# First expert pass gathered from a list made of the ranks alone; gate rows loaded behind the last weights

## The chip, the cores and the metric

The kernel runs on one core of a Trainium2 chip. The metric is the device time of one execution in microseconds (us).

## What is computed

One inference step of a two-layer trunk over 640 tokens (128 context, 512 latent), width 1024, all in fp32. Every layer mixes tokens (mLSTM, windowed attention, neighbourhood attention), adds and normalises, and then runs a mixture of experts:

```python
pg = softmax(x @ w_rg); grp = argmax(pg)            # 1 of 4 groups
top_l, top_i = top_k(le_of_that_group, 2)           # 2 of its 8 experts
out = (silu(xb @ w_g[e]) * (xb @ w_u[e])) @ w_d[e]  # 1024 -> 256 -> 1024, 32 experts
y = segment_sum(out * w, token, 640)
x = layer_norm(ALPHA * x + gate_f * y, g, b)
```

The change lies in the routing and in the start of the experts, once in each layer.

## The kernel before

**The experts.** Each layer streams all 32 experts' weights from HBM: every expert has a gate, an up and a down piece of 1 MB each. Experts 0 to 3 have a fixed place (64 rows each): passes 0 and 1 hold two each. The others are ordered by how many tokens chose them, and passes 2 to 16 take one or two of them each. Last comes a loop for what overflows (one turn in this run) with four experts' pieces. The 96 pieces of a layer go through 18 slots of SBUF in one fixed order. SyncE (SP) issues them all on one DMA queue (`piece`, L752 to L761); before a piece it waits until TensorE is done with the piece that held the slot. Pieces 0 to 11 are those of passes 0 and 1; pieces 12 to 14 wait for the experts' order (`ctl`); piece 15 waits for the token weights (`w12`, made after the token lists) and for the landing of the first gather (`gath0`), since its slot lies over tiles of the routing. Piece 16 is split in two halves. Piece 17 waits for `x1` of the last token tile, which GpSimd makes. Piece 18 and the following wait for passes 0, 1, ... in turn: 18 and 19 for the gates of pass 0, 20 and 21 for its ups, 27 for the downs of pass 1.

**A pass.** For pass b GpSimd gathers 128 token rows from HBM (`gather`, L3016) by a list of token numbers `gidx`, one column a pass; TensorE turns them (`block_x`, L1513), ScalarE and VectorE copy one half each to SBUF, TensorE makes gates and ups (`block_gates_ups`, L1532), turns the hidden values (L1563) and makes the downs (`block_down`, L1553); GpSimd scatters the rows by `sidx` (L3029). In program order TensorE does gates and ups of pass b, then the turning of pass b+1, then the downs of pass b-1.

**The routing,** ahead of pass 0, is one chain between VectorE and TensorE. VectorE picks the experts of the last token tile. TensorE counts (job RK: every token's rank in its expert). VectorE finds which expert outranks which (`outrank`), TensorE sums (RR), VectorE gives each expert its place, TensorE spreads it (RB). VectorE then computes each token's pass and slot (`hot["pass"]`, `hot["slot"]`), TensorE turns these into lists (RX, L1489, 10 matmuls), VectorE makes `gidx` and `sidx` of them (`lists`, L2646 to L2654), TensorE puts `sidx` in order for light passes (RQ, L1498). Between these jobs TensorE runs `keep_busy(16)` twice (L882), matmuls whose result nobody reads. ScalarE fills the gather's target with zeros ("nought", L1910) when all rows of h2, the experts' input, have been stored to HBM (`st_h2`); GpSimd waits for `st_h2`, `nought` and `lists`, then gathers for pass 0 and pass 1. VectorE, after its lists, makes the token weights (`weights_of_two`, L2523 to L2530), one `ln_gain` (L2383) and the overflow numbers (L2667 to L2678).

**The gate rows.** The gate of the second residual, `m["gf"]`, is two rows of 1024 numbers, each broadcast to 128 partitions (512 KB written each). GpSimd loads them in pass PASSES - 2 = 15. They are used after the last pass, in `combine`.

Of the kernel before, what the change touches and what calls it, by code (L numbers as in the profile page):

```python
# [21 lines left out]
P = 128  # L22
# [245 lines left out]
for _stage, _steps in (  # L268
        ("cond", ("sig_c", "silu_c", "maskb", "hmod", "modT", "arows", "arow", "acol")),
# [4 lines left out]
        ("route", ("r_ge", "r_ed", "r_gd", "r_dl", "assign", "hot", "ctl", "outrank", "place", "wx", "logits", "w12"))):  # L274
# [146 lines left out]
def program(nc, A, table):  # L421
    ev = Events(table)
    with ExitStack() as ctx:
# [115 lines left out]
        hot["past"] = region(att, 3524, 1, MAXOVF, NE)  # L539
        s5 = region(small, 0, P, 20, NT)  # L540
# [92 lines left out]
        def x_turned(b_, half):  # L633

            out, src = e["xT"][:, parity(b_), half * 512:(half + 1) * 512], bank[half][:, :]
            if isinstance(b_, int) and b_ < PASSES and pass_kind(b_) == "heavy":
                return out, src
# [80 lines left out]
        def _(eng):  # L718
# [9 lines left out]
            for l in range(DEPTH):  # L728
# [60 lines left out]
                for i in range(12, len(PIECES) - 3 * QUAD):  # L789
# [9 lines left out]
                    elif i == 15:  # L799
                        eng.wait_ge(*ev.at("w12", l))  # L800
# [9 lines left out]
                with eng.Fori(0, more) as i:  # L810
                    src = [expert(i * QUAD + (LOOP0 + c)) for c in range(QUAD)]
                    for q, free in enumerate(("quad_gates", "quad_ups", "quad_downs")):
                        eng.wait_ge(W[free], now(Count(i, 1, 1)))
                        for c in range(QUAD):
                            piece(PASSES, c, q, src[c])
                eng.wait_ge(W["out_psum"], now(Count(more, 1, PASSES)))
# [21 lines left out]
        def _(eng):  # L838
# [145 lines left out]
            for l in range(DEPTH):  # L984
# [489 lines left out]
                last.then_inc(*jobs.filled())  # L1474
                bk = jobs.open("RB", l)
# [6 lines left out]
                keep_busy(16)  # L1482
                bk = jobs.open("RX", l)
                eng.wait_ge(*jobs.room())
                for k in range(2):
                    eng.wait_ge(*ev.at("hot", l, k))
                    for t in range(NT):
                        n = k * NT + t
                        last = eng.matmul(bk[:, 0:NLIST], hot["slot"][:, n, :], hot["pass"][:, n, :], start=(n == 0),  # L1489
                                          stop=(n == 2 * NT - 1))  # L1490
                last.then_inc(*jobs.filled())


                bk = jobs.open("RQ", l)
                eng.wait_ge(*jobs.room())
                eng.wait_ge(*ev.at("lists", l))
                for c_ in range(QUAD):
                    last = eng.matmul(bk[c_ * UNIT:(c_ + 1) * UNIT, 0:NLIST], by_entry(ident)[:, 0, c_, :],  # L1498
                                      r["t1"].rearrange("p t n -> p (t n)")[:, 0:NLIST], start=True, stop=True)
                last.then_inc(*jobs.filled())  # L1500
                W = MOE[l]
                for n in range(jobs.n - BANKS, jobs.n):
                    eng.wait_ge(*ev.at("free", n))
# [1618 lines left out]
```

## Time and profile before

| | us |
|---|---|
| three runs | 1553.67, 1550.94, 1554.16 (median 1553.67) |
| profiled execution, its own time | 1554.2 |
| span of the profiled execution | 1552.4 |
| TensorE busy | 1419.2 (91%) |
| VectorE / ScalarE / GpSimd busy | 610.6 / 335.2 / 366.5 |
| granted TensorE clock, mean | 0.963 of full |
| mean DMA rate over the span | 240 GB/s |

The experts' part of layer 0 lies at 485 to 757 us of the span, that of layer 1 at 1236 to 1508. DMA rates in a stretch are given as the mean busy share of the 16 DMA engines and as GB/s. All times below are from the span's start.

### The profile page before, as it was taken

To read this page: it belongs to the slowest core of one execution; us is meant where nothing else is said; L and a number is where in the kernel's file an instruction comes from. 1 tells how busy PE (TensorE), PEld (TensorE's weight loads), DVE (VectorE), ACT (ScalarE), POOL (GpSimd) and SP (SyncE) were. 2 spreads that over 40 slices of the span, in tenths; PEclk is the share of its full clock that TensorE was granted. 3 is DMA by queue.
4 is the path that set the end of the run, shared out by engine and by line. 5 is a ranking of instruction groups with operands and counts; after the bars stand their busy time and mean duration, and the time that the engine had idled before them with its cause. 6 is when DMAs were issued, how large, how long until landed. Compare 5 with 4: busy or idle time off the path is not lost.

```text
span 1552.4 us, 25254 instructions
## 1 busy us (share of the span) xinstructions
PE 1419.2 (91%) x9681; PEld 1089.8 (70%) x9681; DVE 610.6 (39%) x1453; ACT 335.2 (22%) x853; POOL 366.5 (24%) x471
## 2 busy tenths in 40 slices
PE   6999999898998999996899999989888989999974
PEld 5889898675887766563488889876577876656441
DVE  1121333578278322211352124348746852211216
ACT  2211211464111111110141111236420111111102
POOL 0100006542451312111010000744237321121101
PEclk9999999999998999999999999999999989999987
DMA  9420111675817999999642111147442499999974
GB/s 378 129 65 33 65 62 39 214 278 201 329 65 281 373 381 420 418 418 418 248 127 72 58 65 33 68 152 260 172 173 117 164 359 386 420 418 418 417 292 170
DMA packets 76741, 355.37 MB, mean 229 GB/s; under 512 B 20464, under 2 KB 23792, under 8 KB 43088
## 3 DMA queue, kind: packets, MB, share of 16 engines
q1 hardware_dynamic: 43056, 292.66, 47.7%
q0 software_dynamic: 20416, 46.73, 8.3%
q10 hardware_dynamic: 13152, 14.37, 2.8%
q8 instruction: 79, 1.29, 0.3%
q14 instruction: 38, 0.31, 0.1%
HBM read 341.25 MB, written 32.07 MB: 240 GB/s over the span
## 4 chain that ended last, share of the span: by engine, by line
PE 75%; DVE 8%; DMA 8%; issue 4%; POOL 3%; ACT 1%; SPq 1%; ACTq 0%; DVEq 0%; POOLq 0%
PE bank L1167 22%; PE bank L1532 15%; PE bank L1553 7%; DMA ring<-in_w_exp 4%; PE bank L1403 4%; PE bank L956 2%; PE bank L1151 2%; PE bank L1326 2%; PE bank L859 2%; DMA att<-mod_rows 2%; PE bank L1513 2%; PE bank L1300 1%; PE bank L1113 1%; PE bank L1116 1%; PE bank L882 1%
## 5 line engine op out<-in xcount | busy, mean ns | idle before, releaser
L1167 PE MATMUL bank<-ring,hT 128*128 128x256 f32 (+1 forms) x1600 | 340.9, 373 | 1.1 <-DVE z L2243 1.1
L1167 PEld LDWEIGHTS bank<-ring,hT 128*128 128x128 f32 x1600 | 292.9, 191 | 38.1 <-issue 1.6
L1532 PE MATMUL bank<-z,att 128*64 128x256 f32 (+2 forms) x960 | 181.1, 397 | 11.6 <-DMA ring<-in_w_exp 11.2
L1532 PEld LDWEIGHTS bank<-z,att 128*64 128x64 f32 (+2 forms) x960 | 118.7, 151 | 50.2 <-DMA ring<-in_w_exp 12.2
L1403 PE MATMUL bank<-ring,hT 128*128 128x256 f32 x640 | 142.5, 381 | 1.7 <-ACT hT L1839 1.1
L1403 PEld LDWEIGHTS bank<-ring,hT 128*128 128x128 f32 x640 | 120.7, 191 | 17.8 <-issue 2.0
L2694 DVE TENSOR_TENSOR att<-att,bank 128x256 f32<-128x256 f32 x36 | 15.2, 421 | 273.2 <-ACT att L1928 273.2
L3029 POOL DMA_INDIRECT expert_rows<-att,cur x36 | 37.1, 1031 | 358.5 <-DVE att L2707 349.4
L1532 PE MATMUL bank<-ring,att 128*64 128x256 f32 (+2 forms) x672 | 117.0, 413 | 3.4 <-issue 1.9
L1532 PEld LDWEIGHTS bank<-ring,att 128*64 128x64 f32 (+2 forms) x672 | 71.1, 146 | 21.2 <-issue 4.1
L2243 DVE COPY z<-bank 128x512 f32<-128x512 f32 (+3 forms) x35 | 20.2, 578 | 152.5 <-PE bank L1167 152.5
L1553 PE MATMUL bank<-ring,att 128*64 128x512 f32 (+2 forms) x240 | 72.8, 597 | 6.8 <-DVE att L2713 4.9
L1687 ACT ACTIVATE z<-bank 128x512 f32<-128x512 f32 (+2 forms) x37 | 19.0, 516 | 266.2 <-PE bank L1167 249.4
L1854 ACT ACTIVATE att<-bank,sm 128x384 f32<-128x384 f32 (+2 forms) x100 | 55.4, 559 | 86.0 <-DVE sm L2308 45.1
L1928 ACT ACTIVATE att<-bank 128x256 f32<-128x256 f32 x36 | 13.8, 383 | 269.2 <-PE bank L1532 269.2
L2707 DVE COPY att<-bank 128x512 f32<-128x512 f32 x36 | 24.9, 692 | 109.6 <-PE bank L1553 109.6
L2305 DVE TENSOR_REDUCE sm<-bank 128x1 f32<-128x384 f32 (+2 forms) x100 | 50.4, 532 | 27.3 <-PE bank L1272 16.3
L1532 PE MATMUL bank<-hT,att 128*64 128x256 f32 (+2 forms) x240 | 51.0, 396 | 7.3 <-DMA z<-in_w_exp 6.9
L2852 POOL TENSOR_TENSOR att<-z,const 128x64 f32<-128x64 f32 x64 | 23.7, 400 | 140.2 <-ACT z L1687 139.1
L1553 PEld LDWEIGHTS bank<-ring,att 128*64 128x64 f32 (+2 forms) x240 | 22.4, 140 | 43.1 <-issue 36.3
L3016 POOL DMA_INDIRECT att<-h_rows,att x36 | 37.7, 1047 | 59.8 <-DVE att L2654 24.3
L1300 PE MATMUL bank<-const,att 128*128 128x128 f32 x284 | 41.4, 280 | 8.4 <-DVE att L2329 7.2
(407 smaller groups left out, 2367.9 us busy)
## 6 DMA issues: line engine op xcount, KB each, us to landing
z<-in_w_exp SPq DMA_DIRECT2D x74, 1024.0 KB, 22.3
ring<-in_w_exp SPq DMA_DIRECT2D x72, 1024.0 KB, 23.0
ring<-in_w_ada SPq DMA_DIRECT2D x41, 1024.0 KB, 6.5
ring<-in_w_in SPq DMA_DIRECT2D x24, 1024.0 KB, 5.0
hT<-in_w_exp SPq DMA_DIRECT2D x24, 1024.0 KB, 28.8
att<-in_w_exp SPq DMA_DIRECT2D x12, 1024.0 KB, 7.4
ring<-in_w_out SPq DMA_DIRECT2D x8, 1024.0 KB, 9.8
z<-expert_rows ACTq DMA_DIRECT2D x16, 512.0 KB, 8.9
```

Source lines behind the costliest of these rows:

```text
L859: last = eng.matmul(ada_ps[32 * j:32 * j + 32, P:P + UN], cond_at(m, 2 * j + kk), w[:, 2 * j + kk, :], start=(m == 0 and kk == 0), stop=(m ...
L956: last = eng.matmul(bk[:, i * UN:(i + 1) * UN], hTv[:, k, t * P:(t + 1) * P], w[:, k, :], start=(i == 0 and k == 0), stop=(k == KD - 1), s ...
L1151: last = eng.matmul(bk[:, i * UN:(i + 1) * UN], hTv[:, k, t * P:(t + 1) * P], ws[n][:, k, :], start=(k == 0), stop=(k == KD - 1))
L1167: last = eng.matmul(bk[:, i * UN:i * UN + nw], hTv[:, k, t * P:(t + 1) * P], w[:, k, 0:nw], start=(k == 0), stop=(k == KD - 1))
L1300: last = eng.transpose(bk[:, j * P:(j + 1) * P], c["p"][:, i % 3, s, j * P:(j + 1) * P], ident)
L1403: last = eng.matmul(bk[:, i * UN:(i + 1) * UN], hTv[:, k, t * P:(t + 1) * P], w[2 * half + i][:, k, :], start=(k == 0), stop=(k == KD - 1))
L1532: last = eng.matmul(bank[2 + j][c * m_:(c + 1) * m_, u * DE:(u + 1) * DE], rows, wv[c][k // 4][:, k % 4, :], start=(k == 0), stop=(k == KD ...
L1553: last = eng.matmul(bank[5 + half][c * m_:(c + 1) * m_, :], e["hmT"][:, j, k * P + c * m_:k * P + (c + 1) * m_], wv[c][k][:, half * 512:(h ...
L1854: eng.activation(c["p"][:, i % 3, s, 0:nk], bk[:, 0:nk], ACT.Exp, bias=sm[:, 0, u:u + 1], accum_out=sm[:, 1, u:u + 1]).then_inc(*jobs.free ...
L2305: eng.tensor_reduce(sm[:, 0, 2 * i + s:2 * i + s + 1], bk[:, 0:nk], AX, ALU.max).then_inc(*dve.step())
L3016: eng.indirect_dma_start(e["xg"][:, j, :], None, h2_dram[l], bass.IndirectOffsetOnAxis(ap=col, axis=0), bounds_check=last_row(b_, NTOK), o ...
L3029: eng.indirect_dma_start(y_dram[l], bass.IndirectOffsetOnAxis(ap=cur[:, 2 + j:3 + j], axis=0), e["ob"][:, j, :], None, bounds_check=last_r ...
```

## The change

- VectorE: `rows_shifted` of the last tile (its sum is the last rows of h2) goes ahead of the copy of RK. After `outrank` four new instructions build `hot["first"]`: for the fixed experts 0 to 3 a token's slot in passes 0 and 1 follows from its rank alone. TensorE's new job RF (5 matmuls of one column) turns the part for pass 0 into a list, and VectorE writes it to `cur[:, 0:1]` (two instructions): this is the event `first_rows`.
- GpSimd's gather of pass 0 takes `cur` in place of `gidx`, and waits for `first_rows` and the first half of `nought`; that of pass 1 waits for the other half and for `lists`.
- TensorE: one of the two `keep_busy(16)` is gone. RX and RQ leave the eight-bank job order and use fixed columns of bank 7. RX (`token_lists`) now stands behind the turning of pass 0, RQ (`lists_in_order`) between its gates and its ups.
- Pass 0's rows are not put in the four-way order of light passes, and ScalarE copies both halves of them.
- VectorE: weights, `ln_gain` and the first two overflow instructions stand ahead of the three that finish `sidx`; the rest of the overflow work follows. The event is now `sidx`.
- SP: piece 15 waits for `sidx` in place of `w12`. ScalarE's sigmoid of pass 0 and the first scatter wait for `sidx` too.
- The gate rows are issued by SP behind the last weight piece.

```diff
                     elif i == 15:
-                        eng.wait_ge(*ev.at("w12", l))
+                        eng.wait_ge(*ev.at("sidx", l))
                         eng.wait_ge(W["gath0"], 16)
...
                             piece(PASSES, c, q, src[c])
+                done, count = after(POOL_OF[l][2])
+                eng.wait_ge(W[done], count)
+                eng.wait_ge(*ev.at("st_modr", l))
+                for g in range(2):
+                    eng.dma_start(m["gf"][:, g, :], rows[at:at + D].partition_broadcast(P))
...
+                bk = jobs.open("RF", l)
+                eng.wait_ge(*ev.at("hot_first", l))
+                for t in range(NT):
+                    last = eng.matmul(bk[:, 0:1], hot["first"][:, t, :, :].rearrange("p c j -> p (c j)"), K["idv"][:, t:t + 1],
+                                      start=(t == 0), stop=(t == NT - 1))
...
                         last.then_inc(W["gu" if u else "gate"], 1)
+                        if u == 0 and isinstance(b_, int) and b_ == 0:
+                            lists_in_order()
...
                 keep_busy(16)
                 block_x(0)
+                token_lists()
                 n = passes(eng, l, one_pass, turn)
...
-                for t in range(NT):
-                    eng.wait_ge(*ev.at("st_h2", l, t))
                 eng.wait_ge(*ev.at("assign", l, 1))
                 for j in range(2):
+                    if j:
+                        for t in range(NT):
+                            eng.wait_ge(*ev.at("st_h2", l, t))
...
+                rows_shifted(NT - 1)
                 bk = jobs.bank("RK", l)
...
-                rows_shifted(NT - 1)
+                place_first = r["th"][:, :, 0:2]
+                for c_ in range(2):
+                    last = eng.scalar_tensor_tensor(out=place_first[:, :, c_], in0=r["rk"][:, 0:NT, c_], scalar=float(c_ * CAP - P),
+                                                    in1=r["ma"][:, :, c_], op0=ALU.add, op1=ALU.mult)
+                for c_ in range(2):
+                    last = eng.tensor_tensor(hot["first"][:, :, c_, :].rearrange("p t (h m) -> p t h m", h=2), ...)
+                last.then_inc(*dve.event("hot_first", l))
...
+                overflow_units()
+                lists_sorted()
+                overflow_turns()
                 n = passes(eng, l, one_pass, turn)
...
+                eng.wait_ge(*ev.at("nought", l, 0))
+                eng.wait_ge(*ev.at("first_rows", l))
                 gather(0)
+                eng.wait_ge(*ev.at("nought", l, 1))
+                eng.wait_ge(*ev.at("lists", l))
                 gather(1)
```

TensorE's order from RR to pass 0's ups, layer 0, before (L1473 RR, L1478 and L1480 RB, L882 keep_busy, L1489 RX, L1498 RQ, L1513 turning, L1532 gates and ups):

```order
L1480 MATMUL bank<-const,att 1x32
L882 MATMUL bank<-const 128x128 x16
L1489 MATMUL bank<-att 128x30 [waits dve_route,bank_free2]
...
L1498 MATMUL bank<-att,const 32x30 [waits bank_free2,bank_free3]
L1498 MATMUL bank<-att,const 32x30 x3
...
L882 MATMUL bank<-const 128x128 x15
L1513 MATMUL bank<-const,att 128x128 [waits gath0_0]
L1513 MATMUL bank<-const,att 128x128 x7
L1532 MATMUL bank<-ring,att 64x256 [waits slot_full2,slot_full3,xT_dve_0,xT_act_0]
L1532 MATMUL bank<-ring,att 64x256 x15
L1532 MATMUL bank<-z,att 64x256 [waits ring_full9,ring_full8]
```

The same stretch now (L893 keep_busy, L1528 turning, L1509 RX, L1516 RQ, L1547 gates and ups):

```order
L893 MATMUL bank<-const 128x128 x15
L1528 MATMUL bank<-const,att 128x128 [waits gath0_0]
L1528 MATMUL bank<-const,att 128x128 x7
L1509 MATMUL bank<-att 128x30 [waits dve_route]
...
L1547 MATMUL bank<-ring,att 64x256 [waits slot_full2,slot_full3,xT_dve_0,xT_act_0]
L1547 MATMUL bank<-ring,att 64x256 x15
L1516 MATMUL bank<-att,const 32x30 [waits dve_route]
L1516 MATMUL bank<-att,const 32x30 x3
L1547 MATMUL bank<-z,att 64x256 [waits ring_full9,ring_full8]
```

RX stood ahead of the first turning; it now stands behind it, and so behind the wait for the first gather; RQ stands behind the gates.

VectorE's order from the end of the lists to the overflow numbers, layer 0, before (L2661 to L2663 finish `sidx`, L2523 to L2530 weights, L2383 `ln_gain`, L2667 on overflow):

```order
L2654 TENSOR_TENSOR att<-att 128x30
L2657 COPY att<-att 1x32
L2661 CAST att<-bank 128x2 [waits bank_full3]
L2662 CAST att<-bank 128x3x3
L2663 CAST att<-bank 128x13
L2523 TENSOR_REDUCE small<-att 128x5 [waits act_route]
...
L2383 TENSOR_TENSOR x<-x,z 128x1024 [waits ld_ln1,act_norm,dve_route]
L2667 TENSOR_TENSOR att<-att,const 1x1280
L2669 TENSOR_REDUCE att<-att 1x40 [waits dve_step]
```

And now (L2708 to L2710 finish `sidx`):

```order
L2700 COPY att<-att 1x32
L2547 TENSOR_REDUCE small<-att 128x5 [waits act_route]
...
L2407 TENSOR_TENSOR x<-x,z 128x1024 [waits ld_ln1,act_norm,dve_route]
L2714 TENSOR_TENSOR att<-att,const 1x1280
L2716 TENSOR_REDUCE att<-att 1x40 [waits dve_step]
L2708 CAST att<-bank 128x2 [waits pe_cond,dve_step]
L2709 CAST att<-bank 128x3x3
L2710 CAST att<-bank 128x13
L2721 TENSOR_SCALAR att<-att 1x40
```

The three casts have moved behind the weights, `ln_gain` and two instructions of the overflow.

## Rows read from the trace of the kernel before

**Rows 1.** Stretches of layer 0: us, busy by engine, clock, DMA share, GB/s

```profile
556.00:640.00 84.00, 83.10 (x537) 50.63 (x537) 16.51 (x33) 10.66 (x20) 16.81 (x23) 1.00 1.02 419
640.00:740.00 100.00, 84.36 (x578) 49.53 (x578) 17.38 (x35) 11.04 (x21) 15.99 (x23) 0.96 1.02 418
745.00:750.00 5.00, 3.57 (x34) 2.00 (x38) 1.37 (x3) 0.60 (x1) 0.00 (x0) 1.00 0.05 18
```

**Rows 2.** Chain that ended last, end of layer 0: start, us, what

```profile
705.29 32.48 DMA ring<-in_w_exp
...
747.74 3.67 PE bank L1553 x32
```

**Rows 3.** SP's issues of pieces, layer 0: start, us from first to last

```profile
496.08 2.00 SPq L761 DMA_DIRECT2D z<-in_w_exp  x3
509.52 0.33 SPq L761 DMA_DIRECT2D att<-in_w_exp  x1
546.64 1.44 SPq L761 DMA_DIRECT2D hT<-in_w_exp  x2
```

**Rows 4.** Stretches of 2 and 4 us in layers 0 and 1, as group 1

```profile
544.00:546.00 2.00, 2.00 (x12) 0.57 (x8) 0.00 (x0) 0.00 (x0) 0.00 (x0) 1.00 0.73 297
546.00:548.00 2.00, 2.00 (x13) 1.48 (x10) 1.02 (x2) 0.60 (x1) 0.00 (x0) 1.00 0.33 66
548.00:550.00 2.00, 2.00 (x11) 1.77 (x10) 0.00 (x0) 0.00 (x0) 1.62 (x2) 1.00 0.85 332
...
1296.00:1298.00 2.00, 2.00 (x11) 0.44 (x7) 0.00 (x0) 0.00 (x0) 0.00 (x0) 1.00 0.64 258
1298.00:1300.00 2.00, 2.00 (x13) 1.79 (x11) 1.02 (x2) 0.60 (x1) 0.30 (x1) 1.00 0.48 92
```

**Rows 5.** Chain, start of layer 0's experts: start, us, what

```profile
500.78 2.40 PE bank L1489 x20
503.20 0.20 DVE att L2646
...
504.05 0.10 DVE att L2654
...
505.15 6.24 PE bank L882 x32
511.38 0.89 PE bank L1513 x8
...
513.81 7.14 PE bank L1532 x64
```

**Rows 6.** GpSimd's timeline, layer 0: start, us, what, idle before it and its releaser

```profile
492.48 0.53 POOL L2805 DMA_DIRECT2D h_rows<-att  x1 [7.80 <-DVE att L2430]
505.10 1.10 POOL L3016 DMA_INDIRECT att<-h_rows,att  x1 [12.09 <-DVE att L2654]
507.95 5.12 POOL L2956 TENSOR_TENSOR x<-x,z 128x1024 f32<-128x1024 f32 x2
```

**Rows 7.** DMA issues at 492 to 493, 505 and 514 to 516: KB, us to landing

```profile
h_rows<-att POOLq DMA_DIRECT2D x1, 512.0 KB, 7.3
...
att<-h_rows,att POOLq DMA_INDIRECT x1, 4.2
...
att<-h_rows,att POOLq DMA_INDIRECT x1, 8.2
```

**Rows 8.** VectorE's timeline, layer 0

```profile
490.98 1.20 DVE L2430 TENSOR_TENSOR att<-att 128x1024 f32<-128x1024 f32 x1
...
505.81 1.22 DVE L2383 TENSOR_TENSOR x<-x,z 128x1024 f32<-128x1024 f32 x1
...
508.46 1.47 DVE L2669 TENSOR_REDUCE att<-att 1x40 f32<-1x1280 f32 x1
```

**Rows 9.** keep_busy alone (TensorE, weight loads, clock, DMA), at either clock

```profile
485.00:488.00 3.00, 2.03 (x16) 1.87 (x16) 1.00 1.03 382
495.00:500.00 5.00, 5.00 (x25) 5.00 (x25) 0.50 1.00 365
```

**Rows 10.** The gate rows' issue in pass 15 of layer 0: KB, us to landing

```profile
z<-mod_rows POOLq DMA_DIRECT2D x2, 512.0 KB, 12.3
```

More of the change, by code:

```diff
@@ L1503, in _, with token_lists, lists_in_order @@
                     eng.wait_ge(*ev.at("free", n))
+                def token_lists():
+                    for k in range(2):
+                        eng.wait_ge(*ev.at("hot", l, k))
+                        for t in range(NT):
+                            n = k * NT + t
+                            last = eng.matmul(list_ps["all"], hot["slot"][:, n, :], hot["pass"][:, n, :], start=(n == 0),
+                                              stop=(n == 2 * NT - 1))
+                    last.then_inc(*pe.event("rx", l))
+                def lists_in_order():
+                    eng.wait_ge(*ev.at("lists", l))
+                    for c_ in range(QUAD):
+                        last = eng.matmul(list_ps["sorted"][c_ * UNIT:(c_ + 1) * UNIT, :], by_entry(ident)[:, 0, c_, :],
+                                          r["t1"].rearrange("p t n -> p (t n)")[:, 0:NLIST], start=True, stop=True)
+                    last.then_inc(*pe.event("rq", l))
                 def block_x(b_):
@@ L2590, in _ @@
                 eng.wait_ge(*dve.last())
+                bk = jobs.bank("RF", l)
+                eng.wait_ge(*jobs.full("RF", l))
+                none = r["th"].rearrange("p t g -> p (t g)")[:, 2:3]
+                eng.tensor_scalar(none, bk[:, 0:1], 0.0, float(FAR), ALU.is_equal, ALU.mult).then_inc(*dve.step())
+                eng.wait_ge(*dve.last())
+                eng.scalar_tensor_tensor(out=cur[:, 0:1], in0=bk[:, 0:1], scalar=-1.0, in1=none, op0=ALU.add,
+                                         op1=ALU.add).then_inc(*jobs.freed("RF", l))
+                ev.table[("first_rows", l)] = ev.table.get(("free", jobs.number(("RF", l))))
                 bk = jobs.bank("RB", l)
@@ L2653, in _ @@
                 eng.tensor_copy(sidx[:, :], lx)
-                eng.tensor_tensor(gidx[:, :], lx, lfar, ALU.add).then_inc(*jobs.freed("RX", l))
-                ev.table[("lists", l)] = ev.table.get(("free", jobs.number(("RX", l))))
+                eng.tensor_tensor(gidx[:, :], lx, lfar, ALU.add).then_inc(*dve.event("lists", l))
                 eng.tensor_copy(hot["inc"], inc[0:1, :])
-                bk = jobs.bank("RQ", l)
-                eng.wait_ge(*jobs.full("RQ", l))
-                lights = lambda ap: ap[:, 2:PASSES].rearrange("p (k i) -> p k i", k=GROUPS)[:, :, 2:5]
```

108 lines of the change are left out of this document (57 added, 51 removed).

## The prediction

> **What bounds the kernel now.** I looked for where the experts' part of a layer ends, then for what starts it. The stretches of layer 0 [rows 1] show the 16 DMA engines at a share of 1.02 and 418 to 419 GB/s from 556 to 740 us, without a break, and at 0.05 from 745. TensorE is busy for 84 of the 100 us from 640 to 740: it waits for weights. The chain that ended last says the same [rows 2]: a transfer issued at 705.29 lands 32.48 us later, and only the last downs (3.67 us at 747.74) come behind the last weights. So from 556 on the layer ends when a fixed number of bytes is through, however early TensorE starts its first pass. What moves the end is idle time of the DMA engines before 556, and bytes that stand ahead of the last weights.
>
> Idle time is in two places. At the start SP issues pieces 12 to 14 at 496.08 and piece 15 only at 509.52 [rows 3]. Later piece 27 is issued at 546.64, when pass 1's downs have freed its slot; the shares around it are 0.73, 0.33 and 0.85 [rows 4]: (0.27 + 0.67 + 0.15) x 2 = 2.2 us idle. There the stream has caught up with TensorE, so a stream that starts late can get back these 2.2 us and no more. In layer 1 it is (0.36 + 0.52) x 2 = 1.8 us.
>
> **The change, part by part.**
>
> *The first gather.* `rows_shifted` (1.20 us at 490.98 [rows 8]) moves ahead of the copy of RK and of three short instructions, 0.85 us earlier (491.0 to 490.1). The last h2 store, issued at 492.48 [rows 6], landed 7.3 us later [rows 7], at 499.8; it should land at 498.9. `first_rows` is no limit: four VectorE instructions and RF's five matmuls end near 495.5. Between its releaser (the lists, 504.15 [rows 5]) and its own start (505.10 [rows 6]) GpSimd's gather took 0.95 us, so the first gather starts at 499.9 and not at 505.1: 5.2 us earlier.
>
> *Its landing.* Before, it took 4.2 us, issued when the weight queue was nearly empty; the third, issued into a full queue, took 8.2 [rows 7]. Now pieces 12 to 14 are issued about 1.7 us later than before, from 497.7 to 499.4, so they are in the queue in front of it. (The trace has no row for the four new VectorE instructions ahead of RB. The smallest in it takes 0.10 us [rows 5], the largest 1.47 [rows 8]; at 5 and 320 columns I take 0.35 each, 1.4, and 0.3 for RF ahead of RB on TensorE.) I take 7.2, nearer to the full queue: 507.1. Bounds: 504.1 and 508.1. TensorE's one `keep_busy`, which now starts near 496 and takes 6.2 us [rows 5], is over by then.
>
> The Trainium skill ("DMA: Bandwidth & Descriptors", "Queues, rings and completion order") says that each DMA engine takes its queues in turn, packet by packet. By that the gather would get about half of 420 GB/s at once and land some 1.3 us later than on an empty queue, near 505.4; piece 15 would be issued 1.7 us earlier in each layer and the sum below would come out 3.4 us lower. The 8.2 us of the third gather are nearer to waiting behind what is queued, so the measured row is used.
>
> *The lists.* TensorE turns pass 0 (0.89 us after 511.38) and then makes RX (2.40 us) [rows 5]. Both rows are at the full clock, 2.4 GHz. TensorE has idled since 502.5 by then, and in the stretch after its last wait of this kind the granted clock was 0.50, 1.2 GHz: there a pass of `keep_busy` took 5.00 / 25 = 0.20 us against 2.03 / 16 = 0.13 [rows 9]. So 3.3 us become up to 5.1; I take 4.3 with hand-overs: RX ends at 511.4. The lists are ready 504.15 - 503.18 = 1.0 later, 512.4.
>
> *The event `sidx`.* This is the added wait. Behind the lists VectorE does weights, `ln_gain` (1.22) and two overflow instructions (1.47 each [rows 8]) before it finishes `sidx`. Before, from the lists (504.15) to the end of L2669 (509.93) it was 5.8 us, of which 0.9 was RQ's wait and the three casts; TensorE's `keep_busy`, which waited for these, began at 505.15 [rows 5]. That leaves 4.9, and with the casts (0.5) `sidx` comes at 512.4 + 5.4 = 517.8. RQ itself stands behind pass 0's gates: 511.4 + half of 7.14 [rows 5] + 0.4 = 515.4, not the last. SP issues piece 15 at about 518.0: **8.5 us later** than at 509.52, though the pass it serves has its rows earlier. Behind it in SP's queue stand all later pieces. Piece 17 also waits for `x1`: GpSimd's two `ln_shift` (5.12 us [rows 6]) behind the second gather, near 519, no later than its turn. Pieces 18 to 21 would have been free at 515 to 520.
>
> *From the wait to the end of the layer.* The 8.5 us are idle time of the queue, less what is absorbed: 2.2 us at piece 27 (1.8 in layer 1), and 0.6 for half of a gather (512 KB at 420 GB/s is 1.25 us), since the second gather now falls into the gap. The downs of pass 1, which free piece 27's slot, stay where they are: pass 0's gates start at 511.4 instead of 513.8, but the third gather now waits for overflow numbers that come after `sidx`, and takes that back. The stream reaches piece 27 near 553, so it isn't TensorE that it waits for. Added: 8.5 - 2.2 - 0.6 = 5.7 in layer 0, 6.1 in layer 1.
>
> *The gate rows.* Their 1.05 MB stood in the stream ahead of the last weights (issued in pass 15, landed in 12.3 us [rows 10]); at 419 GB/s that is 2.5 us in each layer. Behind the last weights they move when the engines are otherwise idle (share 0.05 [rows 1]), and land near 751, before `combine` needs them at 766. If that cover were gone they would cost their 2.5 us again. Gain: 2.5 a layer.
>
> *At nothing:* the dropped `keep_busy` (TensorE waits for the gather anyway), ScalarE's second half of pass 0 (0.6 us, beside RX on TensorE), and RF and the four VectorE instructions for it (1.7 us on the routing chain, which now ends at a wait for the gather; their cost is the later start of pieces 12 to 14, and the queue is still full from piece 11 then, or idles under 1 us, which I leave to the range).
>
> **The sum:** layer 0: 5.7 - 2.5 = +3.2; layer 1: 6.1 - 2.5 = +3.6; together +6.8, against the profiled execution's 1554.2: 1561.0. The median of the runs is 0.5 below that execution, so 1560.5.
>
> Bounds of it: with the first gather landing at 504.1 and the full clock, piece 15 is issued 3.0 + 1.0 earlier, at 514.0, and the sum is 6.8 - 8.0 = -1.2. With 508.1 and the low clock throughout it is 1.0 + 0.8 later: +3.6, so +10.4. That is 1552.5 to 1564.1.
>
> **The rivals.**
>
> *The gap closes (faster).* If piece 15 goes out by 512.4, within the 2.8 us that the later catching-up absorbs, the start costs nothing and only the gate rows are left: -5.0, 1548.7. For it: the gather starts 5.2 us earlier. Against: even at its best the way from landing to `sidx` is 3.3 + 1.0 + 5.4 = 9.7 us, so it would have to land by 502.6, 2.7 us after its start; no row is that short. The point from which it decides is this landing.
>
> *No change.* The early gather finds the queue as the first one did and lands in about 4.2 to 5.5 us. The late `sidx` and the gate rows cancel: -1.2 to +3, 1552.5 to 1556.7. The skill's rule on queues taken in turn would lead here.
>
> *Far slower.* TensorE becomes the bound of the start: a third gather issued behind the late overflow numbers, at 522 instead of 514.85, lands 8.2 us later, at 530 to 532, and holds the turning of pass 2; if that carried through to piece 27 beyond 553, idle time came back there. It would add some 3 us a layer: 1566. Against: that turning stood at 530 before, so it slips by 2 us, and the stream has 6 in hand.
>
> *It doesn't do what it says.* Pass 0 doesn't start earlier, since the gather meets the weights: its gates start at 513 to 514 as before, `sidx` is at 519.5. That is the upper bound, 1564.
>
> **How the numbers follow.** A measurement of this kernel tells about 0.2%, 3.1 us, from no change: below 1550.6 is faster, above 1556.8 slower. The forecast with its upper bound and the doesn't-do-it case has 0.54, far slower 0.06; no change 0.24; faster 0.16, more than the landing time alone would give it, since the stream's catching-up is read from one execution. The range, 1549.0 to 1565.0, takes in the bounds and half of the faster case.
>
> **What would show it.** Right: the first gather starts near 500 and lands near 507; piece 15 is issued at 517 to 519 and behind it no dip of the DMA share at 546; a DMA share far below 1 from about 509 to 519; the last downs of layer 0 some 3 us later; gate rows landing behind the last weights. Wrong: piece 15 before 514, or the gap there and the dip at 546 both still present, or a DMA share under 1 between 560 and 740, which would make TensorE the bound.

## The result, and the profile after

The change makes the kernel slower: median 1569.33 us (1568.51 to 1573.6, 6 runs) against 1552.31 (1549.1 to 1555.16, 6 runs of the kernel before), a ratio of 1.0109 [1.0093, 1.0125], so +17.0 us. Forecast were +6.8 us, and a range that ended at 1565.0. The sign and the wait that costs the time were right. The size was not: three terms of the way to that wait were too small, and one of them left out a cause. The profiled execution took 1569.26 us.

The page's heads, against the table above:

```profile
span 1567.4 us, 25180 instructions
...
PE 1419.2 (91%) x9637; PEld 1084.7 (69%) x9637; DVE 610.6 (39%) x1463; ACT 336.5 (21%) x855; POOL 365.6 (23%) x467
```

No engine has noticeably more work: TensorE's 1419.2 us are the same to the tenth, and ScalarE has 1.3 us more. The 15 us between the two spans are waiting. Stretches of layer 0 after the change (us, busy by engine, clock, DMA share, GB/s), where [rows 1, 4] stood:

```profile
504.00:506.00 2.00, 0.00 (x0) 0.00 (x0) 0.00 (x0) 0.00 (x0) 0.00 (x0) 0.70 1.02 424
...
508.00:522.00 14.00, 14.00 (x87) 10.52 (x88) 8.06 (x17) 1.08 (x2) 6.48 (x3) 0.63 0.08 23
...
550.00:552.00 2.00, 2.00 (x12) 0.77 (x12) 1.14 (x3) 0.60 (x1) 0.00 (x0) 1.00 1.02 424
552.00:554.00 2.00, 2.00 (x11) 0.66 (x8) 0.26 (x1) 0.26 (x1) 0.00 (x0) 1.00 1.03 420
556.00:640.00 84.00, 83.10 (x508) 51.83 (x508) 17.24 (x35) 11.05 (x21) 16.20 (x23) 1.00 1.02 419
640.00:740.00 100.00, 89.67 (x618) 53.38 (x614) 18.05 (x36) 11.65 (x22) 16.97 (x24) 0.98 1.02 418
```

From 556 us on the queue is at 1.02 as in [rows 1], and the stream sets the end of the layer. The dip near piece 27 [rows 4] is gone, as forecast. In its place stands a hole: 14 us at a share of 0.08, from the end of pieces 12 to 14 to piece 15. SP's issues, as [rows 3], with piece 5 (the start of the first row) ahead of them:

```profile
469.45 9.50 SPq L763 DMA_DIRECT2D ring<-in_w_exp  x4
...
496.47 2.00 SPq L763 DMA_DIRECT2D z<-in_w_exp  x3
522.25 0.33 SPq L763 DMA_DIRECT2D att<-in_w_exp  x1
```

In the trace of before piece 5 is issued at 471.56. Nothing of the change lies ahead of it, and over all fourteen profiled executions of this study it lies between 468.95 and 473.04, in no order of theirs. So from here on places are told as distances from piece 5's issue in the same layer. Piece 15 is issued at 38.0 before (509.52 - 471.56) and at 52.8 after in layer 0; at 37.9 and 52.0 in layer 1.

Next, what held `sidx` back. TensorE's timeline of the work that ends in it (start, us, what, idle before it and its releaser):

```profile
507.52 1.97 PE L1528 MATMUL bank<-const,att 128*128 128x128 f32 x8 [5.51 <-DMA att<-h_rows,cur]
509.28 4.31 PE L1509 MATMUL bank<-att 128*128 128x30 f32 x20
513.52 6.08 PE L1547 MATMUL bank<-ring,att 128*64 128x256 f32 x32
519.54 0.33 PE L1516 MATMUL bank<-att,const 128*32 128x30 f32 x8
```

VectorE's and GpSimd's timelines behind the lists:

```profile
515.46 1.23 DVE L2407 TENSOR_TENSOR x<-x,z 128x1024 f32<-128x1024 f32 x1
516.60 3.63 DVE L2714 TENSOR_TENSOR att<-att,const 1x1280 f32<-1x1280 f32 x1
520.27 1.47 DVE L2716 TENSOR_REDUCE att<-att 1x40 f32<-1x1280 f32 x1
...
521.93 0.16 DVE L2710 CAST att<-bank 128x13 int32<-128x13 f32 x1
```

```profile
498.64 1.10 POOL L3066 DMA_INDIRECT att<-h_rows,cur  x1 [8.54 <-issue]
...
516.46 6.00 POOL L3006 TENSOR_TENSOR x<-x,z 128x1024 f32<-128x1024 f32 x2
```

The instruction on 1x1280 numbers with two inputs, as it was before (VectorE's timeline of before):

```profile
506.96 1.47 DVE L2667 TENSOR_TENSOR att<-att,const 1x1280 f32<-1x1280 f32 x1
```

DMA issues at 496 to 500 (KB, us to landing):

```profile
z<-in_w_exp SPq DMA_DIRECT2D x3, 1024.0 KB, 7.4
att<-h_rows,cur POOLq DMA_INDIRECT x1, 8.8
```

The gather starts 29.2 behind piece 5 instead of 33.5, but takes 8.8 us instead of 4.2 and lands at 38.0, where the old one landed (37.8). The change sends the gather off 4.3 us sooner and the rows arrive no sooner; the lists, which used to be made before it, are now made behind it. Turning and RX run at 1.2 GHz (granted clock 0.50; 1.97 and 4.31 us against 0.89 and 2.40 [rows 5]), and the 1x1280 instruction takes 3.63 us against 1.47.

The end of layer 0, chain of waits, as [rows 2]:

```profile
715.36 28.42 DMA ring<-in_w_exp
...
751.16 0.87 PE bank L1528 x8
752.03 1.77 issue
753.80 5.37 PE bank L1570 x32
```

The last downs start at 753.80 instead of 747.74 and, at a granted clock of 0.72, take 5.37 us instead of 3.67. They end 7.8 us later (759.17 against 751.41); in layer 1 they end at 1516.86 against 1501.57, 15.3 later: each layer gives half. Counted from piece 5's issue they end 9.9 us later in layer 0 and 8.5 in layer 1.

### The profile page after: what moved, and what is told of

Same layout as the page of the kernel before. It is cut to its first block, busy times and chain, and to the rows that moved or that the text cites. A ratio compares the mean times of both kernels' runs of the same rounds, so it can differ in the third digit from the quotient of the medians.

```text
span 1567.4 us, 25180 instructions
## 1 busy us (share of the span) xinstructions
PE 1419.2 (91%) x9637; PEld 1084.7 (69%) x9637; DVE 610.6 (39%) x1463; ACT 336.5 (21%) x855; POOL 365.6 (23%) x467
## 4 chain that ended last, share of the span: by engine, by line
PE 73%; DMA 11%; DVE 7%; issue 4%; POOL 3%; SPq 1%; ACT 1%; ACTq 0%; POOLq 0%; DVEq 0%
PE bank L1178 21%; PE bank L1547 13%; PE bank L1570 7%; PE bank L1414 5%; DMA ring<-in_w_exp 4%; PE bank L967 2%; PE bank L1162 2%; PE bank L1337 2%; PE bank L870 2%; PE bank L1528 2%; DMA att<-mod_rows 2%; PE bank L1311 1%; DMA att<-h_rows,att 1%; DMA att<-h_rows,cur 1%; PE bank L1124 1%
## 5 line engine op out<-in xcount | busy, mean ns | idle before, releaser
L1547 PE MATMUL bank<-z,att 128*64 128x256 f32 (+2 forms) x960 | 180.5, 395 | 9.8 <-DMA ring<-in_w_exp 9.4
L1547 PEld LDWEIGHTS bank<-z,att 128*64 128x64 f32 (+2 forms) x960 | 117.6, 151 | 48.6 <-DMA ring<-in_w_exp 10.3
L1547 PE MATMUL bank<-ring,att 128*64 128x256 f32 (+2 forms) x672 | 120.3, 425 | 0.0
L2742 DVE TENSOR_TENSOR att<-att,bank 128x256 f32<-128x256 f32 x36 | 15.2, 421 | 260.4 <-ACT att L1952 260.4
L1547 PEld LDWEIGHTS bank<-ring,att 128*64 128x64 f32 (+2 forms) x672 | 71.8, 150 | 20.5 <-issue 5.4
L1952 ACT ACTIVATE att<-bank 128x256 f32<-128x256 f32 x36 | 13.9, 385 | 256.7 <-PE bank L1547 256.7
L2329 DVE TENSOR_REDUCE sm<-bank 128x1 f32<-128x384 f32 (+2 forms) x100 | 50.4, 532 | 27.9 <-PE bank L1283 16.9
L1547 PE MATMUL bank<-hT,att 128*64 128x256 f32 (+2 forms) x240 | 51.1, 397 | 10.2 <-DMA z<-in_w_exp 9.7
L1528 PE MATMUL bank<-const,att 128*128 128x128 f32 x304 | 43.4, 289 | 16.9 <-DMA att<-h_rows,cur 11.4
L1528 PEld LDWEIGHTS bank<-const,att 128*128 128x128 f32 x304 | 35.7, 147 | 27.1 <-DMA att<-h_rows,cur 11.8
```

Source lines behind the costliest of these rows:

```text
L1528: last = eng.transpose(bank[k // 4][:, (k % 4) * P:(k % 4 + 1) * P], e["xg"][:, j, k * P:(k + 1) * P], ident)
L1547: last = eng.matmul(bank[2 + j][c * m_:(c + 1) * m_, u * DE:(u + 1) * DE], rows, wv[c][k // 4][:, k % 4, :], start=(k == 0), stop=(k == KD ...
L2329: eng.tensor_reduce(sm[:, 0, 2 * i + s:2 * i + s + 1], bk[:, 0:nk], AX, ALU.max).then_inc(*dve.step())
```

## The experiments

Every time is given as a difference from the kernel before: its ratio minus one, times 1554 us. For each kernel the trace gives four numbers, which the table at the end collects: piece 15's issue behind piece 5's; piece 27's; the idle time of the 16 DMA engines (one minus their share) from 3 us behind piece 7's issue to 20 us behind piece 27's; and the landing of the layer's last weights behind piece 5's issue. The idle time is 3.75 us in layer 0 and 3.33 in layer 1 before, 16.7 and 16.5 after. The cuts of code show the main lines of an edit; "..." stands for lines left out.

**The gate rows alone** (`gf_only`): the kernel before, with the two loads taken from GpSimd's pass 15 and issued by SP behind the last weight piece.

```diff
                             piece(PASSES, c, q, src[c])
...
+                eng.wait_ge(W[done], count)
+                eng.wait_ge(*ev.at("st_modr", l))
...
+                for g in range(2):
...
+                    eng.dma_start(m["gf"][:, g, :], ...)
...
```

> The kernel before with one part of the change: the gate rows are issued by SP behind the last weight piece. Stream theory (the end of a layer's experts is when the weight bytes are through): the 1.05 MB leave the stream, 2.5 us a layer, so 5.0 us faster than before, near 1547.5. Rival (the gate rows were hidden before, or now land too late for combine): no difference, or up to 5 us slower if combine waits for them.

Measured: 1547.38 us (10 runs), ratio 0.9956 [0.9943, 0.9969], -6.8 us. The last weights land 2.0 and 2.5 us earlier behind piece 5 (274.1 and 272.3 instead of 276.1 and 274.8). The forecast's 2.5 a layer holds: the time gained 3.4 a layer, with an interval from 2.4 to 4.4.

**The whole change without that part** (`list_only`): after, with the gate rows back in GpSimd's pass 15.

> The changed kernel with the gate rows loaded by GpSimd in pass 15 again. Stream theory: their bytes stand in the stream again, 5 to 6.5 us more than the changed kernel, +22 to +23 over before. Rival (in the changed kernel the gate rows land too late and are part of the loss): faster than the changed kernel.

Measured: 1575.37 us (4 runs), ratio 1.0133 [1.0103, 1.0163], +20.7. The list and its order cost some 21 to 24 us by themselves (24 is after's 16.9 and the 6.8 of the gate rows), and these give back 4 to 7.

**Piece 15 late, nothing else** (`late15`). If the stream sets the layer's end, holding piece 15 back must cost time in the kernel before too, though TensorE's passes stay where they are.

```diff
                     elif i == 15:
                         eng.wait_ge(*ev.at("w12", l))
                         eng.wait_ge(W["gath0"], 16)
+                        eng.wait_ge(W["gate"], 1)
```

> The kernel before with one added wait: SP issues piece 15 only when pass 0's gates are done on TensorE, about 8 us later (46 in place of 38 us behind piece 5). Nothing else is moved: the gather, pass 0 and all of TensorE's order stay. Stream theory: the 8 us are idle time of the queue, 3.3 to 3.8 us of idle time later come back, so about 5 us a layer, +9 to +11 over before. Rival (the changed kernel loses its time on TensorE's way into pass 0): no difference, since that way isn't touched.

Measured: 1562.05 us (7 runs), ratio 1.0051 [1.0034, 1.0069], +7.9. Piece 15 is 8.2 and 8.3 us later; piece 27, which TensorE's downs of pass 1 free, is issued where it was: 75.1 behind piece 5 in both layers, as before (75.1 and 75.2). SP's issues, and the stretches where the dip was:

```profile
515.60 0.33 SPq L761 DMA_DIRECT2D att<-in_w_exp  x1
...
544.54 1.44 SPq L761 DMA_DIRECT2D hT<-in_w_exp  x2
```

```profile
542.00:544.00 2.00, 2.00 (x12) 0.57 (x8) 0.00 (x0) 0.00 (x0) 0.00 (x0) 1.00 1.02 414
544.00:546.00 2.00, 2.00 (x11) 1.58 (x10) 1.02 (x2) 0.60 (x1) 0.03 (x1) 1.00 1.01 412
546.00:548.00 2.00, 2.00 (x12) 1.74 (x10) 0.00 (x0) 0.00 (x0) 1.69 (x2) 1.00 1.05 436
```

No dip is left: the later stream has filled it. The rival, by which TensorE's start is what counts, gives zero and falls. Of 8.2 us of delay 4.4 show up as added idle time, and the last weights land 3.1 and 4.1 us later. So some 4 to 5 us of a delay are absorbed in each layer, more than the 2.8 forecast. One part of that is seen in the issues: piece 18 had to wait for pass 0 anyway, and comes 3.9 later, not 8.2.

**More `keep_busy`** (`warm`): after, with `keep_busy(32)` ahead of the first turning, to fill the wait for the gather.

```diff
-                keep_busy(16)
+                keep_busy(32)
                 block_x(0)
```

> The changed kernel with keep_busy(32) in place of keep_busy(16) ahead of the first gather, so that TensorE doesn't idle before it. Stream theory: turning and RX run at 2.4 GHz, 1.0 + 1.9 us sooner, piece 15 is issued 2.9 us sooner, 5.8 us less in two layers than the changed kernel, so +11 over before. Rival (the time is lost on TensorE itself, at 1.2 GHz): turning, RX and pass 0's gates gain 1.0 + 1.9 + 2.5 us a layer, 10.8 in all, so +6 over before.

Measured: 1566.43 us (4 runs), ratio 1.0087 [1.0052, 1.0122], +13.5, 3.4 less than after. TensorE's timeline, and VectorE's:

```profile
508.09 1.09 PE L1528 MATMUL bank<-const,att 128*128 128x128 f32 x8 [1.87 <-DMA att<-h_rows,cur]
509.02 2.31 PE L1509 MATMUL bank<-att 128*128 128x30 f32 x20
511.27 3.67 PE L1547 MATMUL bank<-ring,att 128*64 128x256 f32 x32
```

```profile
514.35 3.65 DVE L2714 TENSOR_TENSOR att<-att,const 1x1280 f32<-1x1280 f32 x1
```

Turning, RX and gates took 6.9 us in place of 12.1, and piece 15 came only 2.8 (layer 1: 1.4) sooner: behind the lists VectorE's own work sets `sidx`, and in it the 3.65 us are still there. In layer 1 TensorE still idled 2.72 us ahead of the turning, and the clock fell to 1.2 GHz again: RX took 3.28 us and the gates 5.99.

**GpSimd held off VectorE** (`warm_shift`): `warm`, and GpSimd's `ln_shift` waits for `sidx`.

> warm with GpSimd's two ln_shift held back until sidx, so that they don't run beside VectorE's overflow instructions. If they slow VectorE down there, its 1x1280 instruction takes 1.5 us again in place of 3.65, piece 15 goes out 2.1 us sooner than in warm (near 47.9) and the kernel is 3 to 4 us faster than warm, +8 to +9 over before. If they don't: 3.65 us again, and as warm or slower, since piece 17 waits for them.

Measured: 1565.43 us (4 runs), ratio 1.0081 [1.005, 1.0112], +12.6. VectorE's and GpSimd's timelines:

```profile
516.66 1.47 DVE L2714 TENSOR_TENSOR att<-att,const 1x1280 f32<-1x1280 f32 x1
```

```profile
520.08 4.78 POOL L3006 TENSOR_TENSOR x<-x,z 128x1024 f32<-128x1024 f32 x2 [3.58 <-DVE att L2710]
```

The same instruction takes 1.47 us when GpSimd is silent: the 3.63 are GpSimd's doing. The time is no better than `warm`'s. RX came late in this execution: TensorE had idled 3.75 us, RX took 4.31 at the low clock, and the lists begin at 513.69. So piece 15 stands at 50.4 and 49.5 and not at the 47.9 expected, and `x1` now ends later, which holds piece 17 (55.3 and 54.4).

**The casts ahead of the overflow numbers** (`warm_order`): `warm`, with `lists_sorted()` ahead of `overflow_units()`.

> warm with one change of VectorE's order: the three casts that finish sidx stand ahead of both overflow instructions (the sigmoid of pass 0 waits for those). sidx then hangs on RQ, behind pass 0's gates: piece 15 at 45.7 us behind piece 5, in place of 50.0 in warm and 52 in the changed kernel. Stream theory: 4.3 us less a layer than warm, 7 to 9 in all, so +4 to +6 over before. Rival (the place of sidx doesn't matter): as warm, +12.

Measured: 1564.37 us (6 runs), ratio 1.007 [1.0046, 1.0093], +10.9, so half of what was hoped for. In layer 1 piece 15 came at 46.8; in layer 0 at 51.2, since there the turning took 1.96 and RX 4.31 us, which are the rows of the low clock, although the 32 `keep_busy` were in place: they ended 2.52 us ahead of the turning. And the casts hang on RQ, which stands behind the gates.

**RQ directly behind RX** (`rq_ahead`): after, with RQ ahead of pass 0's gates, the casts directly behind the lists, and piece 15 on `w12` again. The sigmoid of pass 0 waits for the overflow sum, here and in `warm_order`, `lists_ahead` and `hold12`.

```diff
                 block_x(0)
                 token_lists()
+                lists_in_order()
...
```

> The changed kernel with RQ directly behind RX (ahead of pass 0's gates), VectorE's three casts directly behind the lists, and piece 15 waiting for w12 again. Stream theory: piece 15 is issued near 516.5 in place of 522.25, 5.8 us sooner, 11.6 us in two layers, so +5.5 over before, although TensorE starts pass 0's gates about 1.5 us later. Rival (TensorE's start of pass 0 is what counts): as the changed kernel or 3 us slower, +17 to +20 over before.

Measured: 1563.42 us (6 runs), ratio 1.0056 [1.0037, 1.0075], +8.7. Piece 15 is still at 49.5 and 49.1: everything behind the gather is still behind the gather. The order inside that tail is worth some 8 us of after's 17, not the whole. The rival (+17 to +20) falls. Piece 15 was expected near 47, and VectorE's timeline shows what is missing, the last instruction of the token weights, ahead of `w12`, slowed beside GpSimd:

```profile
518.28 2.88 DVE L2553 TENSOR_TENSOR small<-small 128x5 f32<-128x5 f32 x1
```

On as many numbers it takes 0.17 us in after.

**Lists ahead of the wait for the gather** (`lists_ahead`): the early gather stays, but RX and RQ go back ahead of the first turning, with the second `keep_busy(16)` behind them. The casts and piece 15's wait for `w12` are as in `rq_ahead`.

```diff
                 keep_busy(16)
+                token_lists()
+                lists_in_order()
+                eng.wait_ge(*ev.at("sidx", l))
+                keep_busy(16)
                 block_x(0)
-                token_lists()
...
```

> The changed kernel with RX and RQ ahead of the first turning, made while the first gather is under way, and a second keep_busy(16) behind them; the gather from the ranks alone and the gate rows behind the weights stay. Piece 15 then waits only for the landing of the gather, near 507.7 in the changed kernel's time, as early as before. Stream theory: the whole gap of 14.5 us a layer is gone, only the gate rows' gain is left, and pass 0 starts 1 to 2 us earlier than before, which may move piece 27: 5 to 8 us faster than before, 1545 to 1547.5. Rival (the early gather itself or the 5 us later landing beside pieces 12 to 14 costs the time): slower than before by 5 us or more.

Measured: 1549.95 us (10 runs), ratio 0.9976 [0.9959, 0.9992], -3.7. Undoing the order takes 20 us off after: 12 of them lie between `rq_ahead` and this kernel, that is, in taking the lists out from behind the wait for the gather. Piece 15 is at 39.9 in both layers. The time is 3 us worse than `gf_only`'s (the intervals overlap a little). `gf_only` has no early gather and no list for it, and its pieces 12 to 14 come 2.7 and 2.9 us sooner: the early gather as such brings nothing. VectorE's timeline shows the GpSimd contention at another victim:

```profile
507.78 0.19 DVE L2553 RECIPROCAL small<-small 128x5 f32<-128x5 f32 x1
508.00 2.90 DVE L2555 TENSOR_TENSOR small<-small 128x5 f32<-128x5 f32 x1
```

and GpSimd's what it met:

```profile
508.51 2.36 POOL L3007 TENSOR_TENSOR x<-x,z 128x1024 f32<-128x1024 f32 x1
```

**The gather on an empty queue** (`hold12`): `lists_ahead`, and pieces 12 to 14 wait for the first gather's landing.

> lists_ahead with pieces 12 to 14 held back until the first gather has landed. Two things are told apart. The landing: the gather starts near 29.5 us behind piece 5; with an empty queue it should land 4.2 us later, near 34, in place of 39.8, so pass 0 starts 5 us sooner than in lists_ahead; if the queue isn't what delays it, it lands at 38 to 40 again. The end: by the stream theory the queue idles from 25 to 35 us, the weights reach piece 27 no sooner than in lists_ahead, so its time is that of lists_ahead or up to 6 us more, though TensorE is 5 us ahead; by the rival (TensorE's start counts) it is 8 to 10 us faster than lists_ahead.

Measured: 1551.67 us (10 runs), ratio 0.9979 [0.9963, 0.9994], -3.3. The gather's DMA issue, and SP's issues of the pieces held:

```profile
att<-h_rows,cur POOLq DMA_INDIRECT x1, 4.1
```

```profile
507.67 2.00 SPq L763 DMA_DIRECT2D z<-in_w_exp  x3
513.12 0.33 SPq L763 DMA_DIRECT2D att<-in_w_exp  x1
```

Landing takes 4.1 us and not 8.8: it is the weights in front that make the gather slow. The traces of after and of this kernel split the 4.7 us between them. The gather's first packet starts 4.2 us behind its issue, here 1.8; from there to the landing it is 4.6 us, here 2.3. DMA queues of after, 499 to 502.9 us and 503 to 506 us (q1 has the weights, q0 the gather; packets, MB, share of the 16 engines):

```profile
q1 hardware_dynamic: 219, 1.66, 101.0%
q0 software_dynamic: 1, 0.00, 0.3%
...
q1 hardware_dynamic: 130, 0.93, 73.9%
q0 software_dynamic: 108, 0.35, 28.6%
```

Up to 502.9 us a single packet of the gather moves. Then both queues move side by side, and the gather gets 27% of the bytes. Whether earlier rows would then start pass 0 earlier was not put to the test: TensorE was held by `sidx` and its `keep_busy` until 514.8. The time is that of `lists_ahead`.

**Less `keep_busy` in the kernel with the gate rows moved** (`gf_kb10`): `gf_only`, with the second `keep_busy` cut from 16 to 10. A try for a version better than both.

> gf_only with the second keep_busy cut from 16 to 10, since the gather of the kernel before lands 1.7 us before that keep_busy ends. In gf_only the stream catches up with TensorE at piece 27, so there TensorE's downs of pass 1 set the end: pass 0 starts 1.7 us sooner and the end of each layer's experts too, 3.4 us in all, near 1544; rival: the clock is at 1.2 GHz longer and takes it back, or the end doesn't hang on piece 27, no difference from gf_only.

Measured: 1552.77 us (12 runs), ratio 0.9992 [0.9976, 1.0008]: a miss, it loses most of what the gate rows gained. TensorE's and VectorE's timelines:

```profile
507.80 1.09 PE L1522 MATMUL bank<-const,att 128*128 128x128 f32 x8 [0.59 <-DMA att<-h_rows,att]
512.09 6.58 PE L1541 MATMUL bank<-ring,att 128*64 128x256 f32 x32 [3.19 <-issue]
```

```profile
509.25 2.14 DVE L2687 CAST att<-att 1x42 int32<-1x42 f32 x1
511.31 0.67 DVE L2698 COPY att<-bank 128x512 f32<-128x512 f32 x1
```

The turning ended earlier, but the gates start where they start in `gf_only`, 42.2 us behind piece 5: VectorE's half of the copy waits behind a cast of 42 numbers that takes 2.14 us beside GpSimd's `ln_shift`. The time saved went into TensorE's wait (3.19 us; 2.55 in `gf_only`). In layer 0 the gates then ran at 1.2 GHz for the most part (6.58 us; 3.67 in layer 1), and the last weights land 1.4 us later than in `gf_only`; in layer 1 they land 0.3 sooner. That is 1 of the 5.6 us between the two kernels; the rest is not in this trace, and I can't say where it comes from.

**Both halves to ScalarE** (`gf_act16`: `gf_only`, ScalarE copies both halves of pass 0, VectorE none, and the sigmoid of pass 0 waits for a `ctl` event as well) and **the same with `keep_busy(10)`** (`gf_act10`).

```diff
+                    if isinstance(b_, int) and b_ == 0:
+                        out, src = x_turned(b_, 1)
+                        eng.activation(out, src, ACT.Copy).then_inc(W["xT_dve"], 1)
...
-                evac_x(0)
```

> gf_only with both halves of pass 0's turned rows copied by ScalarE, in place of one by VectorE behind its overflow work. Pass 0's gates start 0.3 us sooner at most, since the turning itself stands behind keep_busy: no difference from gf_only, 6 to 7 us faster than before.

> gf_act16 with the second keep_busy cut from 16 to 10. In gf_kb10 the turning was 2 us sooner, but VectorE's copy behind its overflow work held the gates back. With ScalarE making both copies the gates should start 1.7 to 2 us sooner than in gf_only. If piece 27, and so TensorE, sets the end: 3 to 4 us faster than gf_only, near 1544. If the lower clock takes it back: as gf_only or slower, like gf_kb10.

Measured: 1546.98 us (12 runs), ratio 0.9958 [0.9944, 0.9973], and 1546.09 (12 runs), ratio 0.996 [0.9945, 0.9975]. Both beat the kernel before and the changed one; neither can be told from `gf_only`. In `gf_act10` piece 27 goes out 3.0 and 2.1 us sooner than in `gf_only` and the last weights land 2.8 and 1.7 sooner, but the expected 3 to 4 us did not come.

All of them, in us, layer 0 / layer 1. "By idle" is the added idle time of both layers, less 6.8 where the gate rows stand behind the weights (so `gf_only`'s own row is no test of it). "By landing" is how much later the last weights land than before, both layers together; nothing is taken off it:

| kernel | piece 15 | piece 27 | DMA idle | last weights | by idle | by landing | measured |
| --- | --- | --- | --- | --- | --- | --- | --- |
| before | 38.0 / 37.9 | 75.1 / 75.2 | 3.8 / 3.3 | 276.1 / 274.8 | 0 | 0 | 0 |
| after | 52.8 / 52.0 | 84.5 / 81.2 | 16.7 / 16.5 | 284.3 / 283.3 | +19.3 | +16.7 | +16.9 |
| list_only | 52.9 / 52.3 | 84.6 / 80.8 | 16.4 / 15.9 | 286.7 / 286.0 | +25.2 | +21.8 | +20.7 |
| warm | 50.0 / 50.6 | 78.8 / 81.6 | 13.7 / 14.1 | 281.1 / 282.5 | +13.9 | +12.7 | +13.5 |
| warm_shift | 50.4 / 49.5 | 83.9 / 84.3 | 13.8 / 13.3 | 281.8 / 281.6 | +13.2 | +12.5 | +12.6 |
| warm_order | 51.2 / 46.8 | 84.0 / 79.9 | 15.2 / 10.7 | 282.5 / 278.1 | +12.0 | +9.7 | +10.9 |
| rq_ahead | 49.5 / 49.1 | 82.4 / 81.0 | 13.2 / 13.3 | 280.8 / 281.2 | +12.6 | +11.2 | +8.7 |
| late15 | 46.2 / 46.2 | 75.1 / 75.1 | 8.1 / 7.8 | 279.2 / 278.9 | +8.8 | +7.3 | +7.9 |
| lists_ahead | 39.9 / 39.9 | 76.6 / 76.7 | 5.7 / 5.3 | 275.2 / 273.7 | -2.9 | -2.0 | -3.7 |
| hold12 | 40.1 / 39.9 | 76.9 / 76.7 | 7.2 / 7.5 | 274.5 / 274.1 | +0.8 | -2.3 | -3.3 |
| gf_only | 38.0 / 37.8 | 76.8 / 75.1 | 3.9 / 3.2 | 274.1 / 272.3 | -6.8 | -4.5 | -6.8 |
| gf_kb10 | 38.1 / 38.0 | 78.0 / 75.1 | 5.1 / 3.3 | 275.5 / 272.0 | -5.5 | -3.4 | -1.2 |
| gf_act16 | 38.0 / 38.2 | 74.7 / 73.9 | 2.7 / 2.0 | 271.9 / 271.4 | -9.2 | -7.6 | -6.5 |
| gf_act10 | 38.1 / 38.0 | 73.8 / 73.0 | 2.5 / 1.9 | 271.3 / 270.6 | -9.5 | -9.0 | -6.2 |

For the kernels that lose, the time follows the idle time of the DMA engines at the start, from 0.4 to 4.5 us below it. `warm`, `warm_shift` and `warm_order` are too near each other for their intervals to part them. For small differences it is no guide: `hold12`, `gf_kb10`, `gf_act16` and `gf_act10` lie 2.7 to 4.3 us off it, on either side. The landing of the last weights is the better one: after's 17 us are all in it, and no kernel lies more than 2.8 us off. What is left over is no more than single traces differ by elsewhere: from layer 0's last weights to layer 1's piece 5 it is 471.5 us in `late15`, 476.4 in `gf_only` and 478.6 in `gf_act10`.

## Why the prediction was right and wrong

**What bounds the kernel:** right. A stream that ends 8 us later at an unchanged share of 1.02, and `late15`, which costs 7.9 us with TensorE's piece 27 in its place, show it.

**The first gather starts at 499.9:** nearly. 28.3 behind piece 5 was forecast, 29.2 measured. Pieces 12 to 14, in front of it, come 2.5 us later than before and not 1.7.

**It lands 7.2 us later:** this is the first mis-sized term. 8.8 us, over the upper bound of 8.2; landing was forecast 35.5 behind piece 5 and is 38.0. I had seen that pieces 12 to 14 would stand in front, and still chose a value between two rows. With them issued from 496.47 to 498.47, 3 MB that land 7.4 us after their issue, the gather at 498.64 could hardly land before them. `hold12` shows 4.1 without them. The rival that took the gather to land as the first one did (no change) falls. The estimate from the quoted rule was 1.3 us over an empty queue; measured are 4.7. The rule is that a DMA engine takes its queues in turn, packet by packet (the Trainium skill, "DMA: Bandwidth & Descriptors", "Queues, rings and completion order"). The trace agrees with it from 503 us on: in the first microsecond 34 packets of 4 KB of the gather start beside 36 of 8 KB of weights, and to 506 us 85 beside 114. What failed is the estimate, which gave the gather half of the bytes, where it gets 27%, and let it start at once, where its first packet moves 2.4 us later than on the empty queue. Why it starts so late no run shows.

**Turning and RX take 4.3 us:** the second. They took 6.1 us (507.52 to 513.59), at 1.2 GHz throughout. I had named both clocks and taken the middle; the low clock lasted from before 508 to 518. RX's end slips by 1.8 us more.

**From the lists to `sidx` 5.4 us:** the third, and the one that no bound held. It took 7.5 us, 2.1 more, which is the 1x1280 instruction at 3.63 instead of 1.47. Before, the 1x1280 instruction with two inputs had begun, at 506.96, when `ln_shift` started at 507.95 [rows 6]; the contention fell on the cast of 42 numbers behind it (2.15 us), for which SP doesn't wait. Now both hang on the late lists, the instruction starts just behind `ln_shift`, and it stands ahead of `sidx`. `warm_shift` shows the cause. The Trainium skill has this as a rule ("SBUF — State Buffer", "Who interferes with whom"): a VectorE instruction with two inputs in SBUF and a GpSimd instruction that reads SBUF exclude each other, and whichever starts first keeps the port to its end. The trace agrees: GpSimd began at 516.46, 0.14 us ahead, its instruction takes 2.36 (the row of `lists_ahead`), and 516.46 + 2.36 + 1.47 is 520.29 against a measured end of 520.23. Which of the two starts first is less plain in `lists_ahead`: there VectorE's instruction on 128x5 starts at 508.00, ahead of `ln_shift` at 508.51, and still ends with it (510.90 and 510.87); what GpSimd had under way at 508.00 was the issue of its second gather. The prediction had no term for this.

Together: 0.9 + 1.6 + 1.8 + 2.1 = 6.4 us, and piece 15, forecast at 46.4 behind piece 5, is at 52.8. **The 8.5 us were 14.8**, in layer 1 14.1; there too the 1x1280 instruction took 3.65 us, and turning and RX ran at 1.2 GHz (1.97 and 4.31). RQ, forecast at 515.4 and "not the last", ran at 519.54 and was still not last (the overflow sum ended at 521.74), but by 1.9 us only: the low clock held it and the contention held VectorE, side by side, which is why `warm` and `warm_shift` each gained less than their own term.

**The wait's absorption, 2.2 + 0.6:** the mechanism was right (no dip at 546), and the size not far off: 14.8 us of delay became 13.0 of added idle time, an absorption of 1.8, while in `late15` it was near 4. The last weights land 8.2 and 8.5 us later, and these 16.7 us are the time lost. The way to them from the idle time has a gap: 13.0 less 2.0 to 2.5 for the gate rows would be some 10.7, and the 2 us between I can't assign.

**The gate rows, 2.5 a layer:** right (`gf_only`). They land a little later than was said: in after's layer 0 the first half at 752.99, just ahead of the last weights (753.71), the second at 756.19, where 751 was forecast.

**Costing nothing:** the dropped `keep_busy` was not free. TensorE idled 5.51 us ahead of the turning and then ran on the low clock; filling a part of the wait is worth some 3 us (`warm`, whose interval overlaps with after's). And the last downs at a clock of 0.72 in layer 0 (+1.7) were not foreseen either.

**The sum:** two layers with 6.4 us more delay each make +6.8 into +19.6, against 17.0 measured. The 2.6 us too much are part of the 2 us a layer that stay unassigned.

**The range** ended at 1565.0, since its upper bound moved landing and clock by 1.8 us together and had nothing in it for an instruction made slower by another engine. Of the rivals, "it doesn't do what it says" describes best what happened: pass 0's gates begin 44.1 behind piece 5, where they began 42.3 before (513.81 - 471.56). Its price was too low by the same terms. "Far slower" came nearest in number, for a wrong reason: TensorE does not bound the stretch up to piece 27, as the shares of 1.00 to 1.03 from 530 to 556 show.

**Open:** where `gf_act10` loses again the 4.5 us by which its last weights land sooner than `gf_only`'s (in the profiled executions the stretch between the layers is 2.2 longer); why `gf_kb10` is so slow; what makes the clock fall behind one short wait and not behind another; why the gather's first packet starts late; the 2 us above.

## What to carry to other kernels

If a transfer stream sets the end, look for the event on which its issue hangs, and move no work ahead of that event that waits for something else: here an output that came early was tied to one that then came late. Putting the lists back ahead of the wait was worth 12 us, and 20 together with the order behind them. A transfer that is issued sooner but behind bulk traffic arrives no sooner. When VectorE's instructions are reordered, hold each against what GpSimd does at that moment: the price of one can rise by a whole GpSimd instruction.

## What the runs showed that I had not expected

- A VectorE instruction on 128x5 numbers took 2.90 us instead of 0.17 (`lists_ahead`), a cast of 42 numbers 2.14 (`gf_kb10`) instead of 0.18 (after), and one on 1x1280 3.63 instead of 1.47, each beside a GpSimd instruction on 128x1024. GpSimd pays as well: its two `ln_shift` took 6.00 us in after, 5.12 before [rows 6], 4.78 with VectorE's two overflow instructions out of the way.
- A gather of 512 KB takes 4.1 us with the queue of weights empty and 8.8 with 3 MB in front, though it is issued by GpSimd and they are by SP: its first packet starts 4.2 us behind the issue instead of 1.8, and then shares the engines with them.
- In after TensorE idled 5.51 us and ran its next matmuls, without a break, at 1.2 GHz from 507.5 to about 518 us. In `warm` it was at 2.4 GHz behind an idle time of 1.87 us. In `warm_order`, with the same 32 `keep_busy`, it was not behind 2.52 us (turning 1.96 us); in `warm_shift` the turning behind 3.75 us was still fast (1.18 us), and RX behind it slow (4.31).
